# Attention steps that fill a bank of 512 score columns

## The chip, the cores and the metric

One core of a Trainium2 chip runs the whole program. The metric is device time in microseconds for one launch, the median of several executions. The engines are named as the profile names them: PE (TensorE, matrix products), PEld (its weight loads), DVE (VectorE), ACT (ScalarE), POOL (GpSimd), SP (SyncE, which issues the weight transfers).

## The reference, cut to what matters

512 tokens of width 1024 pass through two stacks of layers in float32: projections, attention, output projection, feed-forward. Four of the sublayers hold attention with heads of 64 columns, or 256 in the cross attention to a memory of 256 tokens:

```python
p = softmax(mask(q @ k.T * scale))      # per head and query: the maximum, the exponentials, their sum
o = (p * gate) @ v                      # gate: a factor per query in the first layer, else 1
```

All but the cross attention are causal: a tile `t` of 128 queries (t = 0 to 3) sees `(t + 1) * 128` keys. The first layer holds three kinds of heads: "sel" and "win" (both causal; their mixes and those of a third branch over compressed keys are added up in one bank) and "B" (a window of 128 keys, hence 128 or 256 score columns, and a sink logit that joins the sum). The second layer is causal with 16 heads, the third ("forget") causal with 8 heads and a second product that is added to the scores.

## The kernel before, in words

Each linear layer keeps 128 rows of output in a PSUM bank and adds 24 products of 128x512 for it (w_hi by x_hi, w_hi by x_lo, w_lo by x_hi, L604 to L606). Attention is a list of *steps*, made by `steps_layer0` (48 steps, called U0 here), `steps_causal` (U1 with 32 steps, UF with 16) and `steps_memory` (UX with 8, used twice). A step holds a pair of *units*, two heads with the same query tile. A unit has `nk` score columns (128 to 512), and owns one of three score banks (`S_BANKS`), one of eight buffers `pr` and a slot of `negm`, `den` and `wgt`. A *group* is all that ends up in one bank of mixes: one query tile, four pairs of heads.

The engines run the same loop, with an iteration `s` for each step and four more to drain (`TURN, LAG = 3, 4`). In iteration `s` each does the following, in this order:

- PE: scores of step s (L771), which wait until DVE has taken unit 0 of step s-1 out of its bank (`sm_done`); transposes of step s-3 (L792), which wait for POOL and for the copies of the step ahead; mixes of step s-4 (L806).
- DVE: mask and negated maximum of both units (L1721), copy of unit 0's transposes (L1731), reciprocals of the sums of step s-1 (L1735); if step s-4 ended a group, `split_mix` waits for ACT's half and writes the low part (L1701).
- ACT: exponentials of unit 0 (L1201), copy of unit 1's transposes (L1235), exponentials of unit 1; if step s-4 ended a group, `split_mix` writes the high part (L1194).
- POOL: weights the exponentials by reciprocal and gate (L566), one instruction for each unit.

`in_turns` orders the steps: wide and narrow query tiles alternate, 512 columns and then 128 (tiles 3 and 0), 384 and then 256 (tiles 2 and 1). Hooks put further work at the end of given iterations. In U0 it is the compressed branch: scores on PE (L914), mask and maximum on DVE (L1883 to L1887), exponentials on ACT (L1359), weights on DVE (L1894 to L1899), transposes on PE (L925), a copy on ACT (L1365), once for each tile, at the iterations that the `CMP_` tuples list. In UF the hooks are a conversion on ACT (L1498) and a subtraction on DVE (L2101) in iterations 4 to 7. The scores of the first two or three steps are placed into the value projection ahead (`BEGUN0`, `BEGUN`).

Of the kernel before, what the change touches and what calls it, by code (L numbers as in the profile page):

```python
# [156 lines left out]
def two_stacks(nc, x_in, mem_in, weights, small_in, tables_in, rope_in, cmpmask_in, sel_dram, out):  # L157
# [3 lines left out]
    with ctx:  # L161
# [26 lines left out]
        den = sb("den", [P, 4, 2])  # L188
        negm = sb("negm", [P, 4, 2])
        wgt = sb("wgt", [P, 4, 2])  # L190
# [159 lines left out]
        def step(group, two, opens=True, closes=True):  # L350
            return dict(group=group, two=two, opens=opens, closes=closes, begins=False, ends=False)
# [9 lines left out]
        def in_turns(couples, banks):  # L361


            steps = []
            for x, y in couples:
                assert len(x) == len(y)
                for two in zip(x, y):
                    steps += two
            for s, st in enumerate(steps):
                names = [o["group"]["name"] for o in steps]  # L370
                st["begins"] = st["group"]["name"] not in names[:s]
                st["ends"] = st["group"]["name"] not in names[s + 1:]
            free = [(0, b) for b in banks]
            n = 0
            for st in steps:
                if st["begins"]:
                    st["group"]["after"], st["group"]["bank"] = free.pop(0)
                if st["ends"]:
                    st["group"]["number"] = n
                    n += 1  # L380
                    free.append((n, st["group"]["bank"]))
            return steps
# [4 lines left out]
        def steps_layer0():  # L387
# [17 lines left out]
            def main(t):  # L405
                g = new_group(t, 0)
                return [step(g, pair(branch, t, j), branch == "sel", False)
                        for j in range(4) for branch in ("sel", "win")]

            def other(t):  # L410
                g = new_group(t, 1)
                return [step(g, pair("B", t, j)) for j in range(4)]

            return in_turns([(main(3), main(0)), (main(2), other(0) + other(1)),
                             (main(1), other(2) + other(3))], (4, 5))

        def steps_causal(q, k, v, halves, scale, banks, forget=False):
            def group(t, half):
                g = new_group(t, half)
                steps = []  # L420
                for i in range(4):
                    two, j = [], 4 * half + i
                    for b in range(2):
                        rows = slice(b * HD, (b + 1) * HD)
                        qk = [(q[rows, j, tokens(t)], k[rows, j, 0:(t + 1) * P])]
                        if forget:
# [4 lines left out]
                    steps.append(step(g, two))  # L431
                return steps

            return in_turns([(group(a, half), group(b, half))
                             for a, b in ((3, 0), (2, 1)) for half in range(halves)], banks)

        def steps_memory(banks):
            def group(t, half):
# [8 lines left out]
                return [step(new_group(t, half), two)]  # L447

            return in_turns([(group(t, 0), group(t, 1)) for t in range(TB)], banks)
# [24 lines left out]
        def ended(steps, t, half):  # L474
            return [s + 1 for s, st in enumerate(steps) if st["ends"] and st["group"]["name"] == (t, half)][0]
# [38 lines left out]
        def _(pool):  # L514
# [42 lines left out]
            def attention(steps):  # L557

                for st in steps:
                    n = pairs_seen.next() - 1  # L560
                    pool.wait_ge(wgt_ready, n + 1)
                    for a, u in enumerate(st["two"]):
                        p = pr[:, (2 * n + a) % 8, 0:u["nk"]]
                        w = wgt[:, n % 4, a:a + 1]
                        gate = ones[:, 0:1] if u["gate"] is None else u["gate"]
                        nc.gpsimd.tensor_scalar(p, p, w, gate, ALU.mult, ALU.mult).then_inc(pn_ready, 1)  # L566
# [23 lines left out]
        def _(pe):  # L590
# [170 lines left out]
            def scores(steps, s0, s):  # L761
                two = [(u, 2 * (s0 + s) + a) for a, u in enumerate(steps[s]["two"])]
                for u, n in two:
                    if n >= 3:
                        pe.wait_ge(sm_done, n - 2)

                parts = len(two[0][0]["qk"])
# [1616 lines left out]
```

## Time and profile before

| | |
|---|---|
| median of 3 runs | 2790.15 us (2788.83 to 2790.53) |
| profiled execution | 2791.02 us, its span 2789.1 us |
| PE busy in the span | 2721.9 us (98%) |
| DVE, ACT, POOL busy | 1020.7, 1099.2, 1269.6 us |
| attention phases U0, U1, UF (with their drain) | 114.2, 73.6, 41.4 us |

The span runs from the first instruction to the last; the execution's own time has 1.9 us more around it. A matmul's end is modelled in the profile and overlaps the start of the next, so a step of PE is read from the start of one kind of work to the start of the next. A float32 product of scores or mixes has two records, a transpose one.

### The profile page before, as it was taken

The page shows a single profiled execution, that of the slowest core. Times are in us where ns is not written, and L with a number is a line of the kernel's source. Part 1 is how long each engine was busy: PE and PEld are TensorE (multiplying, and loading weights), DVE is VectorE, ACT ScalarE, POOL GpSimd, SP SyncE. Part 2 cuts the span into 40 slices and gives each one's busy share as a digit, 9 for nine tenths or more (in the row PEclk, how much of TensorE's full clock was granted, in tenths as well). Part 3 has the DMA queues.
Part 4 walks back from the last instruction along what each step waited for, and adds up shares of the span by engine and source line. Part 5 has one row for each costly group of instructions (what it writes and reads, how often), then busy time and mean ns, then how long its engine had stood idle before and what let it go on. Part 6 is the DMA issues. An engine that isn't in the chain of part 4 may idle for free.

```text
span 2789.1 us, 37598 instructions
## 1 busy us (share of the span) xinstructions
PE 2721.9 (98%) x13426; PEld 2223.8 (80%) x13426; DVE 1020.7 (37%) x1931; ACT 1099.2 (39%) x1791; POOL 1269.6 (46%) x713
## 2 busy tenths in 40 slices
PE   8999999999999999999999999999999999999997
PEld 6856888888867888888868888888887788888886
DVE  5565322214544322105544335222037652422202
ACT  7565323224564333223254334323237443433321
POOL 3544444444444444444544634444444463454442
PEclk9999999999999999999999999999999999999999
DMA  4300222233211222332312412232322341132231
GB/s 165 127 2 32 90 103 92 98 106 102 98 39 50 98 98 91 105 106 76 109 42 102 146 43 83 91 104 95 108 75 99 105 153 46 62 112 98 91 109 63
DMA packets 69222, 252.08 MB, mean 90 GB/s; under 512 B 7680, under 2 KB 7936, under 8 KB 68864
## 3 DMA queue, kind: packets, MB, share of 16 engines
q1 hardware_dynamic: 68112, 247.43, 25.9%
q10 hardware_dynamic: 1008, 3.28, 0.4%
q8 instruction: 65, 1.06, 0.2%
q14 instruction: 37, 0.30, 0.0%
HBM read 248.58 MB, written 2.10 MB: 90 GB/s over the span
## 4 chain that ended last, share of the span: by engine, by line
PE 89%; DVE 6%; ACT 3%; issue 1%; DMA 0%; POOL 0%; DVEq 0%; SPq 0%; POOLq 0%; ACTq 0%
PE ps L604 25%; PE ps L605 25%; PE ps L606 25%; PE ps L771 3%; PE ps L806 3%; PE ps L792 2%; PE ps L713 1%; PE ps L715 1%; PE ps L714 1%; DVE ps L1973 1%; DVE x L1977 1%; DVE xl L1629 1%; DVE pr L1721 1%; PE ps L1013 1%; PE ps L1014 1%
## 5 line engine op out<-in xcount | busy, mean ns | idle before, releaser
L519 POOL TENSOR_TENSOR w_lo<-w_raw,w_hi 128x1024 fp32r<-128x1024 f32 x460 | 1106.7, 2410 | 1305.6 <-ACT w_hi L1133 1297.9
L604 PE MATMUL ps<-xh,w_hi 128*128 128x512 f32 x2260 | 886.7, 392 | 14.2 <-POOL w_lo L519 7.5
L605 PE MATMUL ps<-xl,w_hi 128*128 128x512 f32 x2260 | 881.6, 390 | 0.0
L606 PE MATMUL ps<-xh,w_lo 128*128 128x512 f32 x2260 | 881.3, 390 | 0.0
L1133 ACT ACTIVATE w_hi<-w_raw 128x1024 fp32r<-128x1024 f32 x462 | 485.3, 1055 | 534.3 <-PE ps L606 473.8
L604 PEld LDWEIGHTS ps<-xh,w_hi 128*128 128x128 f32 x2260 | 425.5, 188 | 110.2 <-issue 14.7
L606 PEld LDWEIGHTS ps<-xh,w_lo 128*128 128x128 f32 x2260 | 425.5, 188 | 88.7
L605 PEld LDWEIGHTS ps<-xl,w_hi 128*128 128x128 f32 x2260 | 425.6, 188 | 88.4 <-issue 1.0
L604 PE MATMUL ps<-hh,w_hi 128*128 128x512 f32 x704 | 273.9, 389 | 0.0
L606 PE MATMUL ps<-hh,w_lo 128*128 128x512 f32 x704 | 273.9, 389 | 0.0
L605 PE MATMUL ps<-hl,w_hi 128*128 128x512 f32 x704 | 273.9, 389 | 0.0
L1267 ACT ACTIVATE tmpa<-tmpa 128x512 f32<-128x512 f32 x88 | 55.6, 632 | 427.3 <-DVE tmpa L1671 427.2
L1671 DVE TENSOR_TENSOR tmpa<-ps,rstd 128x512 f32<-128x512 f32 x88 | 60.8, 690 | 385.6 <-PE ps L606 385.6
L1201 ACT ACTIVATE pr<-pr,negm 128x512 f32<-128x512 f32 (+2 forms) x224 | 120.1, 536 | 101.7 <-DVE negm L1721 101.6
L606 PEld LDWEIGHTS ps<-hh,w_lo 128*128 128x128 f32 x704 | 132.2, 188 | 27.6
L604 PEld LDWEIGHTS ps<-hh,w_hi 128*128 128x128 f32 x704 | 132.2, 188 | 27.6
L605 PEld LDWEIGHTS ps<-hl,w_hi 128*128 128x128 f32 x704 | 132.2, 188 | 27.0
L566 POOL TENSOR_SCALAR pr<-pr,wgt,ones 128x256 f32<-128x256 f32 (+3 forms) x160 | 91.3, 581 | 118.7 <-DVE wgt L1735 118.7
L1721 DVE CUSTOM_DVE_ANT_0 pr<-ps,tab 128x512 f32<-128x512 f32 (+2 forms) x192 | 85.7, 477 | 113.0 <-PE ps L771 111.7
L1671 DVE TENSOR_TENSOR tmpb<-ps,rstd 128x512 f32<-128x512 f32 x96 | 66.3, 691 | 154.5 <-PE ps L606 154.4
L1781 DVE TENSOR_TENSOR x<-ps,x 128x512 f32<-128x512 f32 x32 | 22.1, 691 | 273.0 <-PE ps L606 273.0
L1760 DVE TENSOR_TENSOR hl<-tmpb,hh 128x512 f32 (+1 forms) x88 | 63.8, 725 | 80.7 <-ACT hh L1271 80.7
(299 smaller groups left out, 2998.9 us busy)
## 6 DMA issues: line engine op xcount, KB each, us to landing
w_raw<-weights_in SPq DMA_DIRECT2D x462, 512.0 KB, 3.2
x<-x_in SPq DMA_DIRECT2D x4, 512.0 KB, 7.3
mem<-mem_in ACTq DMA_DIRECT2D x2, 1024.0 KB, 4.8
x_out<-x SPq DMA_DIRECT2D x4, 512.0 KB, 2.6
rope<-rope_in SPq DMA_DIRECT2D x1, 512.0 KB, 10.1
tab<-tables_in ACTq DMA_DIRECT2D x2, 256.0 KB, 2.7
tab<-tables_in SPq DMA_DIRECT2D x1, 384.0 KB, 10.6
small<-small_in ACTq DMA_DIRECT2D x1, 326.5 KB, 4.7
```

What stands on the lines that cost most here:

```text
L519: nc.gpsimd.tensor_tensor(w_lo[:, slot], w_raw[:, slot], w_hi.bitcast(f32)[:, slot], ALU.subtract).then_inc(lo_ready, 1)
L566: nc.gpsimd.tensor_scalar(p, p, w, gate, ALU.mult, ALU.mult).then_inc(pn_ready, 1)
L604: nc.tensor.matmul(dst, w_hi[:, slot, w], hi, start=first, stop=False)
L605: nc.tensor.matmul(dst, w_hi[:, slot, w], lo, start=False, stop=False)
L606: return nc.tensor.matmul(dst, w_lo[:, slot, w], hi, start=False, stop=last)
L771: last = nc.tensor.matmul(ps[:, S_BANKS[n % 3], 0:u["nk"]], q, k, start=c == 0, stop=c == parts - 1)
L806: last = nc.tensor.matmul(ps[rows, g["bank"], tokens(column)], values[kb], pt[:, (n + a) % 4, tokens(kb)], start=st["opens"] and kb == 0, ...
L1133: A(w_hi[:, s], w_raw[:, s], ACT.Copy).then_inc(hi_ready, 1)
L1201: A(p, p, ACT.Exp, scale=-1.0, bias=negm[:, slot, a:a + 1], accum_out=den[:, slot, a:a + 1]).then_inc(p_ready, 1)
L1671: return V.tensor_tensor(dst, bank[0:rows, 0:n], r[0:rows, 0:n], ALU.mult)
L1721: V.tensor_tensor_reduce(out=pr[:, n % 8, 0:nk], in0=ps[:, S_BANKS[n % 3], 0:nk], in1=u["mask"], scale=-u["scale"], scalar=start, op0=ALU.add,
L1760: V.tensor_tensor(at(hl), tmpb[:, j % 2], at(fp(hh)), ALU.subtract).then_inc(hl_ready, 1)
```

## The change

A step may now hold several *segments*, each a pair of units as before, laid side by side in the banks, as long as together they have at most 512 columns. Each segment keeps its own maximum, sum, reciprocal and bank of mixes, so the score products, mask-and-maximum instructions, exponentials, POOL's weightings and mixes are as many as before and as wide. The transposes of a step, the copies of them (now 512 wide for two segments), the reciprocals and the signals between engines come once for each step. `steps_causal` makes steps of tile 3 alone (512), of tiles 2 and 0 (384 + 128), and of two pairs of tile 1 (256 + 256). `steps_layer0` does the same for "sel" and "win"; "B" units stay alone, since the sink's column follows theirs. There are 37 steps in U0, 20 in U1 and 10 in UF, 29 fewer in all; UX has the same 8.

```diff
+        def step(*segs):
+            at = 0
+            for sg in segs:
+                sg["at"] = at
+                at += sg["two"][0]["nk"]
+            return list(segs)
...
-            return in_turns([(main(3), main(0)), (main(2), other(0) + other(1)),
-                             (main(1), other(2) + other(3))], (4, 5))
+            steps = [step(sg) for sg in m3]
+            steps += [step(m2[0]), step(m2[1])] + [step(m2[i + 2], m0[i]) for i in range(6)] + [step(m0[6], m0[7])]
+            for j in range(4):
+                steps += [step(b0[j]), step(m1[2 * j], m1[2 * j + 1])]
+            for j in range(4):
+                steps += [step(b1[j]), step(b2[j])]
+            return with_banks(steps + [step(sg) for sg in b3], (4, 5))
...
-            return in_turns([(group(a, half), group(b, half))
-                             for a, b in ((3, 0), (2, 1)) for half in range(halves)], banks)
+            for half in range(halves):
+                g0, g1, g2, g3 = (group(t, half) for t in range(TB))
+                for i in range(4):
+                    steps += [step(g3[i]), step(g2[i], g0[i])]
+                steps += [step(g1[0], g1[1]), step(g1[2], g1[3])]
+            return with_banks(steps, banks)
...
-        CMP_ORDER = (3, 0, 2, 1)
-        CMP_SCORES, CMP_MASKED, CMP_EXP = (1, 3, 14, 26), (1, 3, 15, 27), (1, 4, 16, 28)
-        CMP_WEIGHTS, CMP_TURNED, CMP_COPY = (1, 4, 17, 29), (2, 5, 18, 30), (2, 6, 19, 31)
+        CMP_ORDER = (3, 2, 0, 1)
+        CMP_SCORES, CMP_MASKED, CMP_EXP = (1, 4, 8, 14), (1, 4, 9, 15), (1, 5, 10, 16)
+        CMP_WEIGHTS, CMP_TURNED, CMP_COPY = (1, 6, 11, 17), (2, 7, 12, 18), (2, 8, 13, 19)
...
+                for sg in steps[s]:
+                    parts, cols = len(sg["two"][0]["qk"]), slice(sg["at"], sg["at"] + sg["two"][0]["nk"])
+                    for c in range(parts):
+                        for a, u in enumerate(sg["two"]):
+                            q, k = u["qk"][c]
+                            last = nc.tensor.matmul(ps[:, S_BANKS[(n0 + a) % 3], cols], q, k,
+                                                    start=c == 0, stop=c == parts - 1)
+                            if sg is steps[s][-1] and c == parts - 1:
+                                last.then_inc(s_ready, 1)
...
-                            for kb in range(u["nk"] // P):
+                            for kb in range(width(steps[s - TURN]) // P):
...
+                for i, sg in enumerate(steps[s]):
+                    u = sg["two"][a]
+                    p = pr[:, n % 8, sg["at"]:sg["at"] + u["nk"] + (u["sink"] is not None)]
+                    last = A(p, p, ACT.Exp, scale=-1.0, bias=negm[:, slot, i, a:a + 1],
+                             accum_out=den[:, slot, i, a:a + 1])
+                last.then_inc(p_ready, 1)
...
-                    if s >= LAG and steps[s - LAG]["ends"]:
-                        split_mix(steps[s - LAG]["group"], hi, lo)
+                    for sg in steps[s - LAG] if s >= LAG else []:
+                        if sg["ends"]:
+                            split_mix(sg["group"], hi, lo)
```

PE's queue in U1, early in the phase, before: wide and narrow steps alternate, each with its scores (L771), transposes (L792) and mixes (L806).

```order
L771 MATMUL ps<-k_r,q_r 128x512 x2
L792 MATMUL ps<-ident,pr 128x128 x2
L806 MATMUL ps<-pt,v_t 64x128 x8
L771 MATMUL ps<-k_r,q_r 128x128 x2
L792 MATMUL ps<-ident,pr 128x128 x8
L806 MATMUL ps<-pt,v_t 64x128 x2
```

The same place in the changed kernel (the lines are L793, L814 and L829 now).

```order
L793 MATMUL ps<-k_r,q_r 128x384 x2
L793 MATMUL ps<-k_r,q_r 128x128 x2
L814 MATMUL ps<-ident,pr 128x128 x8
L793 MATMUL ps<-k_r,q_r 128x512 x2
L814 MATMUL ps<-ident,pr 128x128 x8
L829 MATMUL ps<-pt,v_t 64x128 x8
```

Every run of transposes and of mixes has now eight, where it had two or eight, and a second pair of score products stands directly behind the first.

DVE's queue in U1 where the first two groups end, before: each `mix_l` stands between the reciprocals of one iteration and the mask instructions (printed as ISA) of the next, and the two ends are an iteration apart.

```order
L1731 COPY pt<-ps 128x128
L1735 RECIPROCAL wgt<-den 128x2
L1701 TENSOR_TENSOR mix_l<-ps,mix_h 128x512
L1721 ISA pr,negm<-ps,tab 128x128
L1721 ISA negm 128x1
L1721 ISA pr,negm<-ps,tab 128x128
L1721 ISA negm 128x1
L1731 COPY pt<-ps 128x512
L1735 RECIPROCAL wgt<-den 128x2
L1701 TENSOR_TENSOR mix_l<-ps,mix_h 128x512
```

The same place in the changed kernel, from the second of the ends on; tile 3's group ended an iteration earlier.

```order
L1761 COPY pt<-ps 128x512
L1765 RECIPROCAL wgt<-den 128x2
L1728 TENSOR_TENSOR mix_l<-ps,mix_h 128x512 x2
L1751 ISA pr,negm<-ps,tab 128x512
L1751 ISA negm 128x1
L1751 ISA pr,negm<-ps,tab 128x512
L1751 ISA negm 128x1
```

The groups of tiles 2 and 0 end in the same step, so two `mix_l` stand in a row ahead of the next mask instructions.

DVE's queue at the end of U1, the drain of the last steps, before: all copies of transposes (`pt`) stand ahead of the last two `mix_l`.

```order
L1731 COPY pt<-ps 128x384
L1735 RECIPROCAL wgt<-den 128x2
L1731 COPY pt<-ps 128x256
L1735 RECIPROCAL wgt<-den 128x2
L1731 COPY pt<-ps 128x384
L1731 COPY pt<-ps 128x256
L1701 TENSOR_TENSOR mix_l<-ps,mix_h 128x512 x2
```

And in the changed kernel:

```order
L1761 COPY pt<-ps 128x512
L1765 RECIPROCAL wgt<-den 128x4
L1728 TENSOR_TENSOR mix_l<-ps,mix_h 128x512
L1761 COPY pt<-ps 128x512
L1728 TENSOR_TENSOR mix_l<-ps,mix_h 128x512 x2
L1761 COPY pt<-ps 128x512
L1728 TENSOR_TENSOR mix_l<-ps,mix_h 128x512
```

The last two copies of transposes now stand behind `mix_l` instructions, where they stood ahead of them.

## Rows read from the trace of the kernel before

**Rows 1.** The page, part 4: shares of the chain that ended last, by engine.

```profile
PE 89%; DVE 6%; ACT 3%; issue 1%; DMA 0%; POOL 0%; DVEq 0%; SPq 0%; POOLq 0%; ACTq 0%
```

**Rows 2.** Stretches U0, U1, UF: us; PE, PEld, DVE, ACT, POOL busy (count); clock; DMA.

```profile
138.30:252.50 114.20, 104.73 (x943) 68.59 (x942) 78.92 (x352) 74.76 (x251) 53.30 (x94) 1.00 0.01 5
792.60:866.20 73.60, 67.53 (x601) 43.34 (x600) 46.56 (x186) 50.26 (x158) 35.85 (x60) 1.00 0.01 2
1422.30:1463.70 41.40, 35.14 (x324) 24.16 (x324) 24.93 (x90) 25.63 (x77) 16.72 (x28) 1.00 0.03 5
```

**Rows 3.** PE's waits in U0, U1, UF: sum in us, times, longest.

```profile
PE ps L771 <- DVE negm L1721: 6.1, 7, 2.0
PE ps L925 <- DVE s_c L1899: 1.2, 1, 1.2
PE ps L792 <- DVE pt L1731: 1.0, 4, 0.3
...
PE ps L771 <- DVE negm L1721: 4.6, 6, 0.9
PE ps L792 <- ACT v_t L1220: 0.4, 1, 0.4
...
PE ps L771 <- DVE negm L1721: 5.0, 6, 1.0
```

**Rows 4.** Timeline of PE in U1, without waits: start, us, instructions.

```profile
803.11 1.13 PE L771 MATMUL ps<-k_r,q_r 64*128 64x512 f32 x4
804.17 0.44 PE L792 MATMUL ps<-ident,pr 128*128 128x128 f32 x2
804.53 1.09 PE L806 MATMUL ps<-pt,v_t 128*64 128x128 f32 x16
805.56 0.49 PE L771 MATMUL ps<-k_r,q_r 64*128 64x128 f32 x4
806.04 1.07 PE L792 MATMUL ps<-ident,pr 128*128 128x128 f32 x8
807.03 0.44 PE L806 MATMUL ps<-pt,v_t 128*64 128x128 f32 x4
807.40 1.13 PE L771 MATMUL ps<-k_r,q_r 64*128 64x512 f32 x4
...
826.59 0.92 PE L771 MATMUL ps<-k_r,q_r 64*128 64x384 f32 x4
827.44 0.44 PE L792 MATMUL ps<-ident,pr 128*128 128x128 f32 x2
```

**Rows 5.** Timeline of U1 where the first group ends: start, us, [idle <-releaser].

```profile
809.86 0.49 PE L771 MATMUL ps<-k_r,q_r 64*128 64x128 f32 x4
...
810.29 0.71 ACT L1201 ACTIVATE pr<-pr,negm 128x512 f32<-128x512 f32 x1
...
810.99 0.58 ACT L1194 ACTIVATE mix_h<-ps 128x512 fp32r<-128x512 f32 x1
...
811.33 0.44 PE L806 MATMUL ps<-pt,v_t 128*64 128x128 f32 x4
811.61 0.69 DVE L1701 TENSOR_TENSOR mix_l<-ps,mix_h 128x512 fp32r<-128x512 f32 x1 [1.35 <-ACT mix_h L1194]
812.21 0.28 DVE L1721 CUSTOM_DVE_ANT_0 pr<-ps,tab 128x128 f32<-128x128 f32 x1
...
812.65 1.13 PE L771 MATMUL ps<-k_r,q_r 64*128 64x512 f32 x4 [0.88 <-DVE negm L1721]
```

**Rows 6.** ACT's exponentials in U1 by shape: xcount | busy us, mean ns | idle.

```profile
L1201 ACT ACTIVATE pr<-pr,negm 128x384 f32<-128x384 f32 x16 | 9.7, 609 | 8.1 <-DVE negm L1721 8.1
...
L1201 ACT ACTIVATE pr<-pr,negm 128x128 f32<-128x128 f32 x13 | 5.1, 392 | 1.0 <-DVE negm L1721 1.0
```

**Rows 7.** Timeline of U0, compressed branch: DVE's weights, then PE's transposes.

```profile
149.01 0.42 DVE L1894 TENSOR_REDUCE cst<-s_c 128x8 f32<-128x256 f32 x1 [1.17 <-ACT s_c L1359]
...
150.59 0.44 PE L925 MATMUL ps<-ident,s_c 128*128 128x128 f32 x2 [1.24 <-DVE s_c L1899]
```

More of the change, by code:

```diff
@@ L359, in tokens, with with_banks @@
             return slice(t * P, (t + 1) * P)
[L361 to L372, printed above, removed]
+        def with_banks(steps, banks):
+            segs = [sg for st in steps for sg in st]
+            names = [sg["group"]["name"] for sg in segs]
             free = [(0, b) for b in banks]
             n = 0
[L375 to L379, printed above, removed]
+            for s, sg in enumerate(segs):
+                sg["begins"] = names[s] not in names[:s]
+                sg["ends"] = names[s] not in names[s + 1:]
+                if sg["begins"]:
+                    sg["group"]["after"], sg["group"]["bank"] = free.pop(0)
+                if sg["ends"]:
+                    sg["group"]["number"] = n
                     n += 1
-                    free.append((n, st["group"]["bank"]))
+                    free.append((n, sg["group"]["bank"]))
             return steps
@@ L446, in group @@
                     two.append(unit(qk, MEM, tab[:, 0:MEM], 1 / 16, places))
-                return [step(new_group(t, half), two)]
-            return in_turns([(group(t, 0), group(t, 1)) for t in range(TB)], banks)
+                return step(seg(new_group(t, half), two))
+            return with_banks([group(t, half) for t in range(TB) for half in range(2)], banks)
         U0 = steps_layer0()
@@ L474, in ended @@
         def ended(steps, t, half):
-            return [s + 1 for s, st in enumerate(steps) if st["ends"] and st["group"]["name"] == (t, half)][0]
+            return [s + 1 for s, st in enumerate(steps) for sg in st
+                    if sg["ends"] and sg["group"]["name"] == (t, half)][0]
         block = ctx.enter_context(nc.Block())
@@ L561, in attention @@
                     pool.wait_ge(wgt_ready, n + 1)
[L562 to L566, printed above, removed]
+                    for a in range(2):
+                        for i, sg in enumerate(st):
+                            u = sg["two"][a]
+                            p = pr[:, (2 * n + a) % 8, sg["at"]:sg["at"] + u["nk"]]
+                            w = wgt[:, n % 4, i, a:a + 1]
+                            gate = ones[:, 0:1] if u["gate"] is None else u["gate"]
+                            last = nc.gpsimd.tensor_scalar(p, p, w, gate, ALU.mult, ALU.mult)
+                        last.then_inc(pn_ready, 1)
             pool.wait_ge(lo_ready, FIRST_TILES)
@@ L785, in attention @@
                     if TURN <= s < len(steps) + TURN:
-                        for a, u in enumerate(steps[s - TURN]["two"]):
+                        for a in range(2):
                             n = 2 * (s0 + s - TURN) + a
@@ L815, in attention @@
                         hook()
-                mts.n += 1 + max(st["group"]["number"] for st in steps)
+                mts.n += 1 + max(sg["group"]["number"] for st in steps for sg in st)
             pe.wait_ge(pool_set, 1)
@@ L929, in cmp_transposes, with cmp_values @@
                 return run
-            def cmp_values(st):
-                g = st["group"]
+            def cmp_values(sg):
+                g = sg["group"]
                 i = CMP_ORDER.index(g["t"])
                 pe.wait_ge(cmp_copied, i + 1)
-                for a, u in enumerate(st["two"]):
+                for a, u in enumerate(sg["two"]):
                     rows, j, _ = u["places"][0]
@@ L1230, in copy_turned @@
                         n = 2 * (s0 + s - TURN) + 1
-                        nk = steps[s - TURN]["two"][1]["nk"]
+                        nk = width(steps[s - TURN])
                         act.wait_ge(pt_ready, n + 1)
```

111 lines of the change are left out of this document (56 added, 55 removed).

## The prediction

> **What bounds the kernel now.** I read the chain first: 89% of it is PE's [rows 1], so an engine that gets less to do brings nothing unless PE had waited for it. Then the three stretches in which the change acts. They last 114.2 + 73.6 + 41.4 = 229.2 us, 8% of the span [rows 2]; nothing outside them is touched. In each, DVE, ACT and POOL are busy for 40 to 69% of the time (in U1 46.6, 50.3 and 35.9 of 73.6 us), no weights stream, and the clock is at its full level of 2.4 GHz [rows 2], so neither bandwidth nor clock enters. The waits of PE say what it waits for: 6.1 + 1.2 + 1.0 us in U0, 4.6 + 0.4 in U1, 5.0 in UF, 18.3 us in 25 waits [rows 3]. Modelled ends hide a piece of each: PE's mixes of one block that start at 811.33 would have been over after 0.37 us (so long they take at 807.03), at 811.70, and the next scores start at 812.65, 0.95 us late, where the row shows 0.88 idle [rows 4, 5]. With 0.07 to 0.08 for each of 25, PE loses about 20.3 us.
>
> Where PE doesn't wait, its own sequence sets the pace. A wide and a narrow step take 803.11 to 807.40, 4.29 us, with no idle time [rows 4]. Differences of starts give the pieces: scores of 512 columns 1.06, of 384 0.85, of 128 0.48; transposes of four blocks 0.99, of one 0.36; mixes of four blocks 1.03, of one 0.37 [rows 4].
>
> **Turns.** Three further blocks of transposes cost 0.99 - 0.36 = 0.63, so 0.21 each, and 0.15 of a run is fixed; mixes likewise (0.66 for three, 0.15 fixed). These fixed parts are PE's turn from one kind of work to the next, with its waits. A merged pair of segments has one run of transposes and one of mixes instead of two: 0.30 us less for each of 29 steps that go, 8.7 us. Scores save nothing: each segment brings its own products, 0.85 + 0.48 before and after. Order doesn't alter a sum: the wider second step, whose scores now lengthen the value projection ahead, takes nothing that it didn't take elsewhere.
>
> **Waits at the end of a group.** At 809.86 the group's last mixes give way to the next scores. ACT still does the exponentials of unit 1 (810.29 to 810.99), then mix_h until about 811.57; DVE, held behind it, does mix_l from 811.61 and the next mask from 812.21; at 812.65 PE may go on: 2.79 us [rows 5]. PE had work for one step meanwhile, a narrow one of 1.84 us. The changed kernel has steps of 1.06 + 0.99 + 1.03 = 3.1 us (one segment) or 0.85 + 0.42 + 2.02 = 3.3 us (two). After a step with one segment the same chain, with a mask of 512 instead of 128 columns, is covered.
>
> Two things speak against. First, ACT is later in a step with two segments: its exponentials take 609 + 392 ns for a unit [rows 6] instead of 0.71 us for 512 columns at once [rows 5], 0.28 more, 0.56 for both units, and DVE's two masks add about 0.1. Secondly, two groups end together, which adds a mix_h (0.58, about 0.5 start to start) and a mix_l (0.60) [rows 5]. I lay the queues down from these durations. In U1 the first end (tile 3, behind one segment) is covered but leaves DVE and ACT 0.6 us late. In the next iteration, counted from PE's first scores: mask of unit 0 out at 2.9 instead of 2.3, its exponentials to 4.0, copy to 4.5, exponentials of unit 1 to 5.5, two mix_h to 6.6, the second mix_l to 7.4, the next mask (512) to 8.1. PE wanted that after its own 3.3 and 3.1 us, at 6.4: about 1.8 us with the signals. Tile 1's end, behind two segments, by the same count: 0.55. In the drain the copy of the last transposes stands behind two mix_l; these end 2.05 us after the mixes, the copy at 2.7, and PE has 2.0 us of work: 0.7. The second half's ends all fall into the drain. U1 then waits 3.1 us where it waited 4.6 + 0.4 (v_t, covered now by 1.33 us of scores instead of 0.48) and small ones.
>
> In UF all ends fall into the drain (0.7). There the hooks of iterations 4 to 7 act like an end of a group: DVE waits for ACT behind its exponentials. The first is covered, the other three cost 1.1, 0.7 and 1.4, since each starts late from the one ahead: 3.9 us in all against 5.0 plus small ones.
>
> U0, in order: 0.6 at the start as now; 1.0 in iteration 8, where PE's compressed scores need the copy pc_t, which the tuples put into the same iteration behind ACT's exponentials (mask out at 0.85 + 0.22 + 0.55, exponentials 0.6, copy 0.5, exponentials 0.6, copy 0.4: 3.8 to 3.9, against 2.9 of PE's work); 1.8 in iteration 12, where PE's turned weights need DVE's chain of 1.6 us (149.01 to 150.59 [rows 7]) that stands behind tile 3's mix_l; 1.85 after tile 0's end, since a step of 128 columns follows; 0.85 after tile 1's; 1.15 and 1.0 in the drain. The wait of 1.2 us for s_c [rows 3, 7] is gone, with two iterations more in between. Sum 8.2.
>
> After: 8.2 + 3.1 + 3.9 = 15.2. Before: 20.3, and 1.2 for a handful of waits of 0.3 and less: 21.5. Gain 6.3 us. This is the soft term. Below, I bound it by no gain (every end waits as now), above by all 21.5.
>
> **Others.** POOL keeps its instructions, 35.9 us of them [rows 2] in some 66 us of U1, so it has room. A step's weightings are now done for both segments before one signal; the transposes they feed are three steps later, some 9 us after the scores, and mask, exponentials, reciprocal and weighting take about 7.5. DVE and ACT lose 29 copies and 29 reciprocals each or between them, which nothing waits for. The masks of a second segment write other columns of the same bank, the same instructions as now.
>
> The Trainium skill, "Trainium Kernel Development and Optimization", Best Practices, says that tiling speeds up compute but not the evacuation of PSUM; here that would mean that merging cannot help an attention that DVE and ACT pace. By that rule the sum would be near zero; the trace doesn't bear it out, as both are idle for about a third of each stretch [rows 2]. What it would take is rival (d).
>
> **Sum.** 8.7 + 6.3 = 15.0 us. The profiled execution took 2791.0 us (span 2789.1 and 1.9 around it), 0.9 above the median of 2790.15. The forecast is 2790.15 - 15.0 = 2775.1, rounded to 2775.
>
> **Rivals.**
> (a) Only the turns are saved: the longer chain of ACT and DVE eats what the wider steps cover. For it: two ends in one step, three hooks in a row in UF. Against: the narrow steps behind each end are gone in U1. Then 2790.2 - 8.7, with waits up to 2 us either way: 2779.5 to 2783.5. 20%.
> (b) Nearly all waits go: the queues recover faster than I laid down, two thirds of 21.5 us or more. 2790.2 - 8.7 - 14 or more: 2767.5 and below, to 2760. 12%.
> (c) The turns aren't saved: PE's fixed 0.15 is a matter of something else than of the run, and stays. Against it: runs of one and of four blocks in the same stretch give it for transposes and mixes alike [rows 4]. Only the waits then: 2790.2 - 6.3 = 2784, and no change if the waits stay too. 5%, of which 3% within 0.2%. The TensorE page of the Trainium skill (TensorE: Matmul & The Clock Gate, Back-to-back issue gap) gives one spacing for a stream of loads and products by their width, with no price for a turn; by that rule the first term would be nothing.
> (d) Slower: ACT becomes the pace. One iteration with two segments costs it 2 x (0.61 + 0.39) for the exponentials [rows 6] and a copy of about 0.6, 2.6 us against PE's 3.3. It decides once ACT needs over 3.3 + 0.3, the saved turn, which would take half a microsecond more for each extra exponential than its row has; at 4.1 us the 29 steps with two segments lose 0.8 each, 23 us, and the turns give 8.7 back: 2804. 4%.
> My own forecast, waits between 9 and 19 us: 2769 to 2779. 59%.
>
> **Numbers.** Below 2766 lies about half of (b), above 2783 lie (d), (c) and the edge of (a), in all some 17%: the range is 2766 to 2783; the forecast's own is 2769 to 2779. A measurement of this kernel tells about 0.2% (5.6 us) from no change. Faster by more: 0.93; within: 0.04; slower: 0.03.
>
> **What would show it.** In the trace after: PE's starts in a step of 384 + 128 columns 0.85 + 0.45, 0.99, 1.03, and U1's 20 steps 3.6 us shorter in PE's own work; PE's waits for negm at two places in U1 (about 1.8 and 0.5), three in UF, a wait for pc_t in U0's iteration 8 and for s_c in iteration 12; a wait for the copy pt in each drain. The stretches U0, U1, UF about 109.5, 66.5 and 37 us (now 114.2, 73.6, 41.4). Wrong would be: transposes waiting for POOL in every iteration, exponentials back to back on ACT (then d), or waits for negm in each of the ends (then a).

## The result and the profile after

| | before | after |
|---|---|---|
| time, median (lowest to highest) | 2789.8 us (2788.8 to 2790.5) | 2824.6 us (2821.4 to 2827.0) |
| profiled execution, span | 2789.1 us | 2821.8 us |
| PE busy | 2721.9 us | 2763.1 us |

The changed kernel is slower: 1.0123 times the time of before, with an interval of 1.0110 to 1.0136. The forecast was 2775 us, the range ended at 2783.

I look first where the change acts. The three attention phases from their first scores to their last mixes, in the windows view of the kernel before (us; busy time and count of PE, PEld, DVE, ACT, POOL; granted clock; DMA):

```profile
124.50:250.88 126.38, 117.43 (x1031) 80.80 (x1029) 85.17 (x377) 78.31 (x261) 59.12 (x98) 1.00 0.03 10
773.08:864.72 91.64, 85.99 (x682) 56.92 (x681) 48.61 (x198) 59.01 (x175) 45.42 (x67) 1.00 0.07 24
1402.30:1462.00 59.70, 53.96 (x410) 38.12 (x409) 26.92 (x102) 33.88 (x94) 26.27 (x35) 1.00 0.10 35
```

And of the changed kernel:

```profile
123.03:245.19 122.16, 113.34 (x1031) 83.28 (x1029) 82.04 (x356) 77.29 (x250) 59.93 (x98) 0.99 0.03 10
780.38:863.34 82.96, 79.97 (x682) 58.41 (x681) 46.20 (x175) 57.57 (x163) 45.21 (x67) 1.00 0.08 26
1413.46:1468.47 55.01, 51.09 (x410) 38.63 (x409) 25.97 (x91) 32.97 (x88) 27.08 (x35) 1.00 0.11 38
```

They are 4.2 + 8.7 + 4.7 = 17.6 us shorter, a little more than the 15.0 of the forecast. So the loss, 32.7 us of span, lies elsewhere, and it must be about 50 us. Between the phases the same instructions run: U1 begins 7.3 us later although U0 ended 5.7 us earlier. The costliest groups on the page of the changed kernel (busy us, mean ns of one, idle) show where:

```profile
L626 PE MATMUL ps<-xh,w_hi 128*128 128x512 f32 x2260 | 899.4, 398 | 12.6 <-POOL w_lo L538 7.3
L628 PE MATMUL ps<-xh,w_lo 128*128 128x512 f32 x2260 | 898.5, 398 | 0.0
L627 PE MATMUL ps<-xl,w_hi 128*128 128x512 f32 x2260 | 883.6, 391 | 0.0
...
L626 PE MATMUL ps<-hh,w_hi 128*128 128x512 f32 x704 | 279.1, 397 | 0.0
```

On the page of before the same lines read:

```profile
L604 PE MATMUL ps<-xh,w_hi 128*128 128x512 f32 x2260 | 886.7, 392 | 14.2 <-POOL w_lo L519 7.5
L606 PE MATMUL ps<-xh,w_lo 128*128 128x512 f32 x2260 | 881.3, 390 | 0.0
...
L604 PE MATMUL ps<-hh,w_hi 128*128 128x512 f32 x704 | 273.9, 389 | 0.0
```

These are the dense linear products, whose code the change doesn't touch. Their count is the same and their idle time is no longer than before; each simply takes longer. Since matmuls overlap, I measure the distance from one product's start to the next. PE's timeline of the changed kernel in a dense stretch (start, us):

```profile
999.86 0.40 PE L626 MATMUL ps<-xh,w_hi 128*128 128x512 f32 x1
1000.09 0.39 PE L627 MATMUL ps<-xl,w_hi 128*128 128x512 f32 x1
1000.32 0.40 PE L628 MATMUL ps<-xh,w_lo 128*128 128x512 f32 x1
...
1001.95 0.39 PE L626 MATMUL ps<-xh,w_hi 128*128 128x512 f32 x1
```

Nine products in 2.09 us are 232 ns each. Over the whole trace the medians behind the three kinds of product (xh with w_hi, xl with w_hi, xh with w_lo) are 234, 230 and 235 ns, where before had 227, 227 and 226. Summed over every pair of neighbouring dense products the distances grow from 2383.8 to 2436.2 us: 52.4 us. 52.4 - 17.6 - 1.5 (the first scores start 1.5 us earlier) = 33.3, against 32.7 in the spans. The account closes to 0.6 us.

The granted clock over the span is 0.993 and 0.994, the mean DMA rate 90 and 89 GB/s: neither accounts for 50 us. What does differ for these products is where their operands lie. The diff makes den, negm and wgt 32 bytes longer each, and all buffers allocated behind them (xh, y_dn, hh, hl, mix_h, pr, pt and the rest, but not x, w_raw, w_hi, w_lo and xl) move up by 96 bytes per partition. In the program built from before, xh lies at 121984 and w_hi at 49280, a distance of 142 x 512; in the changed one it is 96 more.

### The profile page after: what moved, and what is told of

The parts are those of the page before. It is cut to its first block, busy times and chain, and to the rows that moved or that the text cites. A ratio compares the mean times of both kernels' runs of the same rounds, so it can differ in the third digit from the quotient of the medians.

```text
span 2821.8 us, 37279 instructions
## 1 busy us (share of the span) xinstructions
PE 2763.1 (98%) x13426; PEld 2226.9 (79%) x13426; DVE 1008.7 (36%) x1873; ACT 1093.8 (39%) x1762; POOL 1272.0 (45%) x713
## 3 DMA queue, kind: packets, MB, share of 16 engines
q8 instruction: 65, 1.06, 0.2%
## 4 chain that ended last, share of the span: by engine, by line
PE 90%; DVE 5%; ACT 3%; issue 1%; DMA 0%; POOL 0%; DVEq 0%; SPq 0%; POOLq 0%; ACTq 0%
PE ps L626 26%; PE ps L628 26%; PE ps L627 25%; PE ps L793 3%; PE ps L829 2%; PE ps L814 2%; PE ps L735 1%; PE ps L736 1%; PE ps L737 1%; PE ps L1037 1%; PE ps L1038 1%; PE ps L1036 1%; ACT pr L1226 1%; DVE pr L1751 0%; DVE ps L2004 0%
## 5 line engine op out<-in xcount | busy, mean ns | idle before, releaser
L626 PE MATMUL ps<-xh,w_hi 128*128 128x512 f32 x2260 | 899.4, 398 | 12.6 <-POOL w_lo L538 7.3
L628 PE MATMUL ps<-xh,w_lo 128*128 128x512 f32 x2260 | 898.5, 398 | 0.0
L1226 ACT ACTIVATE pr<-pr,negm 128x384 f32<-128x384 f32 (+5 forms) x224 | 119.5, 535 | 89.7 <-DVE negm L1751 89.7
L1751 DVE CUSTOM_DVE_ANT_0 pr<-ps,tab 128x384 f32<-128x384 f32 (+3 forms) x192 | 83.4, 476 | 106.2 <-PE ps L793 105.5
```

The source lines that it names most:

```text
L626: nc.tensor.matmul(dst, w_hi[:, slot, w], hi, start=first, stop=False)
L628: return nc.tensor.matmul(dst, w_lo[:, slot, w], hi, start=False, stop=last)
L1226: last = A(p, p, ACT.Exp, scale=-1.0, bias=negm[:, slot, i, a:a + 1], accum_out=den[:, slot, i, a:a + 1])
L1751: last = V.tensor_tensor_reduce(out=pr[:, n % 8, cols], in0=ps[:, S_BANKS[n % 3], cols], in1=u["mask"], scale=-u["scale"], scalar=start, o ...
```

## The experiments

Theory A: the places of the buffers slow the dense products. Rivals: B, the changed program's instructions are fetched otherwise; C, the shorter attention shifts the weight stream against the products. All experiments but the last two are about this. A *grain* is the number of bytes of which a shift must be a multiple to cost nothing. The distances behind each product are collected in one table below.

### e1 to e4: shifts of 128, 96, 64 and 32 bytes

e1 is the changed kernel, e2 to e4 the kernel before, each with one unused tile. For e2:

```
         stat = sb("stat", [P, 3, TB])
+        pad = sb("pad", [P, 24])
```

e1 has `[P, 8]`, e3 `[P, 16]`, e4 `[P, 4]`. In the built programs every buffer starts at a multiple of 32 bytes, so e4's tile of 16 bytes moves xh and all behind it by 32 (xh lies at 122016): e4 tests a shift of 32 bytes, and no run tests one of 16.

> The changed kernel with one unused tile of 32 bytes per partition allocated behind stat, so that every buffer behind it (xh, hh, hl, pr, mix_h and the rest) stands 128 bytes, not 96, beyond its place in the kernel before; no instruction is added. Theory A (the 32-byte shift of these buffers against multiples of 64 slows the dense products: 227 ns from one product's start to the next became 231 to 237): the products return to 226 to 227 ns, the roughly 50 us they lost come back, and the time is about 2772 to 2776 us, near the 2775 of the prediction. Theory B (the changed program's instructions stand elsewhere and are fetched otherwise) and theory C (the shorter attention shifts the weight stream against the products): nothing of that is touched, the time stays at 2821 to 2827 us and the spacing at 231 to 237 ns.

> The kernel before with one unused tile of 96 bytes per partition behind stat, which puts xh and all buffers behind it at the places they have in the changed kernel; no instruction differs. Theory A: the products slow to 231 to 237 ns apart and the time rises by what the changed kernel lost outside attention, 34.8 + 18 = about 50 us: 2835 to 2845 us. Theories B and C: 2789 to 2791 us, no change.

> The kernel before with an unused tile of 64 bytes behind stat: the buffers behind it move, but each keeps its place against multiples of 64. Theory A with a grain of 64 bytes: no change, 2790 us, products 227 ns apart. Theory A with a grain of 128 bytes: slower, by up to 50 us. Theories B and C: 2790 us.

> The kernel before with an unused tile of 16 bytes behind stat. Theory A with a grain of 32 or 64 bytes: slower, by about as much as with 96 bytes (2835 to 2845 us). If only a grain of 16 bytes or less counts: 2790 us. Theories B and C: 2790 us.

Measured: e1 2801.5 us (1.0046 of before, 1.0031 to 1.0060), e2 2845.2 (1.0207, 1.0190 to 1.0224), e3 2848.8 (1.0216, 1.0196 to 1.0237), e4 2836.8 (1.0173, 1.0153 to 1.0194). An unused tile of 96 bytes makes the kernel before over 50 us slower, without any other instruction: B and C are out as the main cause. The page of e2 has the product lines of the changed kernel, to the nanosecond:

```profile
L605 PE MATMUL ps<-xh,w_hi 128*128 128x512 f32 x2260 | 899.0, 398 | 12.2 <-POOL w_lo L520 6.4
L607 PE MATMUL ps<-xh,w_lo 128*128 128x512 f32 x2260 | 898.5, 398 | 0.0
L606 PE MATMUL ps<-xl,w_hi 128*128 128x512 f32 x2260 | 883.7, 391 | 0.0
```

But my theory of multiples of 64 is wrong. A shift by 64 costs as much as one by 96, and the changed kernel at 128 regains less than half (23 us). A grain of 32, 64 or 128 bytes is out with e4, e3 and e1; it is coarser. (The forecast for e4 took its shift for one of 16 bytes.)

### e5: the changed kernel with every other buffer in its old place

```
-        den = sb("den", [P, 4, 2, 2])
+        den_gap = sb("den_gap", [P, 4, 2])
...
+        den = place("den", [P, 4, 2, 2], 88.25)
```

The same for negm and wgt (88.5 and 88.75).

> The changed kernel with den, negm and wgt moved to free memory behind all other buffers, and gaps of their old size left in their old places, so that every other buffer stands exactly where it stands in the kernel before. Same instructions as the changed kernel. Theory A2 (the places of the product operands against each other or against some coarser grain set the spacing of the dense products, and not whether they are multiples of 64 bytes): the spacing is 226 to 227 ns again and the time is the span of before, 2789.1, less the 17.7 us that the three attention stretches gained, so 2771 to 2774 us. Rival B (the changed program's code slows the products): spacing 231 to 237 ns and 2822 us, or with a part of both something between, above 2780.

Measured: 2770.1 us, 0.9933 of before (0.9920 to 0.9947). The instructions of the changed kernel in the old places gain 20.6 us. The products are as before:

```profile
L630 PE MATMUL ps<-xh,w_hi 128*128 128x512 f32 x2260 | 885.1, 392 | 14.1 <-POOL w_lo L542 7.9
L632 PE MATMUL ps<-xh,w_lo 128*128 128x512 f32 x2260 | 880.4, 390 | 0.0
...
L630 PE MATMUL ps<-hh,w_hi 128*128 128x512 f32 x704 | 273.9, 389 | 0.0
```

and its timeline has six products in 1.36 us, 227 ns each:

```profile
1000.10 0.39 PE L630 MATMUL ps<-xh,w_hi 128*128 128x512 f32 x1
...
1001.46 0.39 PE L630 MATMUL ps<-xh,w_hi 128*128 128x512 f32 x1
```

Rival B gets nothing: summed, the distances between dense products are 2379.7 us, where before had 2383.8. Of the 20.6 us the three phases account for 15.9 in the profiled executions; most of the rest (4.9 us) lies ahead of the first scores, a stretch that took 119.6 us here and 124.5 in before, but 120.0 in e10, which has the instructions of before.

### e6 to e8: one region alone, all together, 512 bytes

In the kernel before: e6 has 96 unused bytes behind y_dn (only hh, hl, mix_h, pr and their region move), e7 64 bytes ahead of x (all buffers move), e8 512 bytes behind stat.

```
         y_dn = sb("y_dn", [P, KT, T])
+        pad = sb("pad", [P, 24])
```

> The kernel before with 96 unused bytes between y_dn and the region of hh: xh keeps its place, hh, hl, mix_h, pr and everything in that region move by 96 bytes. Theory A2, with the effect tied to the operand that moved: the xh and xl products stay at 226 to 227 ns (their sum 1544 us), the hh, hl, mix and y products go to 231 to 237 ns, which costs 6 us a group of hh and hl times three less some, about 14 us, and 2 to 3 us for mix and y: 2804 to 2808 us. If instead any move of any buffer unsettles all products: 2835 us or more.

> The kernel before with 64 unused bytes ahead of x: all buffers move by 64 bytes together, so their distances from each other stay. With 64 bytes behind stat alone the time had been 2848.8 us. If the distance between the moving operand and the weights (or the two read streams against each other) counts: 2790 us, 227 ns. If the place itself against a fixed grain of the memory counts: slower, up to 2849 us.

> The kernel before with 512 unused bytes behind stat. With a grain of 512 bytes or a divisor of it that is at least 256: 2790 us. With a coarser grain, or none (the spacing follows the whole place): slower, between 2800 and 2850 us.

Measured: e6 2806.4 us (1.0059, 1.0040 to 1.0077), e7 2790.6 (1.0000, 0.9990 to 1.0010), e8 2789.6 (0.9997, 0.9987 to 1.0007). On e6's page the x products keep their time and those of hh don't:

```profile
L605 PE MATMUL ps<-xh,w_hi 128*128 128x512 f32 x2260 | 885.2, 392 | 14.3 <-POOL w_lo L520 7.8
...
L607 PE MATMUL ps<-hh,w_lo 128*128 128x512 f32 x704 | 280.9, 399 | 0.0
L606 PE MATMUL ps<-hl,w_hi 128*128 128x512 f32 x704 | 277.4, 394 | 0.0
```

So the effect stays with the products whose operand moved. Moving everything by 64 costs nothing where moving a part by 64 costs some 60 us: for this shift it is the distance between buffers that counts, not the place itself.

### e9, e10, e13, e15: which distances, and the grain

In the kernel before: e9 has 96 bytes between w_hi and w_lo, e13 96 bytes between w_raw and w_hi, e15 96 bytes ahead of w_lo and 160 behind it, e10 256 bytes behind stat. e15:

```
+        pad = sb("pad", [P, 24])
         w_lo = sb("w_lo", [P, RING, CW], f32r)
+        pad2 = sb("pad2", [P, 40])
```

> The kernel before with 96 unused bytes between w_hi and w_lo: w_lo, xl, xh, hh, hl and all the rest move together, so they keep their distances (multiples of 512 bytes) to w_lo and lose them to w_hi. Theory D (a product is slowed where the weights loaded for the next product stand off a multiple of 512 from the moving operand that streams meanwhile): the spacing behind the xh product with w_hi is slow (231 to 237 ns: the next load is from w_hi), behind the xl product 227 (the next load is from w_lo), behind the xh product with w_lo slow. Rival E (a product's own weights and moving operand count): slow behind both products with w_hi, 227 behind the one with w_lo. Either way two of three products are slowed: 2820 to 2840 us. If neither distance counts: 2790 us.

> The kernel before with 256 unused bytes behind stat; 512 had left the time as it was and 128 had left 28 us of loss in the changed kernel. A grain of 256 bytes: 2790 us, products 227 ns apart. A grain of 512 bytes: slower, between 2800 and 2850 us.

> The kernel before with 96 unused bytes between w_raw and w_hi: w_hi, w_lo, xl, xh, hh, hl and all the rest move together; x and w_raw stay. If only the distances among what TensorE reads count: 2788 to 2792 us, products 227 ns apart. If the distance from w_raw to w_hi and w_lo counts (ScalarE and GpSimd read one and write the other all the time): slower, up to 2845 us.

> The kernel before with 96 unused bytes ahead of w_lo and 160 behind it: only w_lo stands off, everything behind it has moved by 256. Theory D (the weights loaded for the next product against the operand that streams meanwhile): slow only behind the xl product with w_hi, 8 us of loss or less for xl and hl together with 2964 products of 3 to 7 ns: 9 to 20 us, 2800 to 2810 us. Rival E (a product's own weights): slow only behind the xh product with w_lo, the same 9 to 20 us. Rival F (any operand off its place slows all three, since each product's start depends on the one ahead): all spacings above 229 ns, 2815 to 2845 us.

Measured: e9 2831.5 us (1.0153, 1.0134 to 1.0171), e10 2790.7 (1.0007, 0.9996 to 1.0017), e13 2790.8 (1.0002, 0.9992 to 1.0012), e15 2839.7 (1.0179, 1.0159 to 1.0200). Median distance in ns from the start of one product to the start of the next, behind each kind, computed from all of them in each trace:

| kernel | moved against w_hi | xh·w_hi | xl·w_hi | xh·w_lo | hh·w_hi | hl·w_hi | hh·w_lo |
|---|---|---|---|---|---|---|---|
| before | nothing | 227 | 227 | 226 | 227 | 226 | 227 |
| after | xh, hh, hl: 96 | 234 | 230 | 235 | 233 | 237 | 231 |
| e2 | the same | 235 | 230 | 235 | 233 | 237 | 231 |
| e1 | the same, 128 | 232 | 226 | 228 | 232 | 232 | 232 |
| e3 | the same, 64 | 233 | 232 | 231 | 233 | 234 | 233 |
| e4 | the same, 32 | 235 | 232 | 232 | 233 | 234 | 234 |
| e6 | hh, hl: 96 | 227 | 226 | 227 | 231 | 231 | 238 |
| e5, e7, e13 | nothing | 227 | 226-227 | 227 | 226-227 | 226-227 | 227 |
| e8, e10 | xh, hh, hl: 512; 256 | 227 | 226-227 | 227 | 226-227 | 227 | 227 |
| e9 | all others: 96 | 232 | 231 | 231 | 232 | 231 | 231 |
| e15 | w_lo: 96; xl, xh, hh, hl: 256 | 233 | 232 | 233 | 233 | 232 | 232 |

The products run 227 ns apart whenever all that PE reads (w_hi, w_lo, xl, xh, hh, hl) lies multiples of 256 bytes apart (differences of 0, 256 and 512 to the distances of before were tried), and some or all kinds of them slower in every case in which one of these buffers doesn't. e13 says that x and w_raw, which only the converting engines read, don't count, and again that a common shift, of 96 bytes here, is free. Theories D (the load of the next weights) and E (a product's own weights) both expected one slow kind in e15; all six are slow, even the product of xh with w_hi, whose own weights and those loaded for the next product both lie right, and the loss is 51 us, where both had expected 9 to 20. That is what F expected: the whole train of products is slow. Its reason, that each product starts from where the one ahead had left off, is not shown. Nor is the train slow evenly: in e1 the xl products keep 226. On e15's page:

```profile
L606 PE MATMUL ps<-xh,w_hi 128*128 128x512 f32 x2260 | 900.7, 399 | 12.7 <-POOL w_lo L521 7.3
L608 PE MATMUL ps<-xh,w_lo 128*128 128x512 f32 x2260 | 893.0, 395 | 0.0
L607 PE MATMUL ps<-xl,w_hi 128*128 128x512 f32 x2260 | 891.0, 394 | 0.0
```

Which product of three is slow isn't fixed by its kind either. With hh and hl off by 96 bytes, one of the three takes 237 or 238 ns and the others 230 to 232: in the changed kernel it is hl·w_hi in the first two down projections and hh·w_hi in the last two (the medians 233 and 237 of the table mix the two), in e6 hh·w_lo in all. The three together take 700 ns in both, against 680 before. So an offset sets the time of a round of three, and the table's columns shouldn't be read as prices of single kinds; e15 refutes D and E by the size of the loss, not by the columns alone.

The inside of it stays open. The distances behind the products of xh with w_lo have a median of 235 ns in every tenth of the changed kernel, while other engines come and go. That speaks for something between PE's own streams (moving operand and weights) rather than for a collision with ScalarE, GpSimd or DMA, but no run shows it by itself.

### e14: the changed kernel with one line of repair

160 unused bytes behind stat, so that the shift is 256 and not 96.

```
         stat = sb("stat", [P, 3, TB])
+        pad = sb("pad", [P, 40])
```

> The changed kernel with 160 unused bytes behind stat, so that all buffers behind it stand 256 bytes beyond their places of before, where 96 is what the change alone moves them by. With a grain of 256 bytes: products 227 ns apart and 2769 to 2774 us, as with every buffer in its old place. If the changed kernel needs the old places themselves: 2780 us or more.

Measured: 2772.7 us, 0.9937 of before (0.9921 to 0.9954), products 227 ns apart. This is the change as it should be shipped; from 2824.6 us the unused tile brings 52.

### e12: the segments of U1 and UF as steps of their own

On the base of e5:

```
-                    steps += [step(g3[i]), step(g2[i], g0[i])]
-                steps += [step(g1[0], g1[1]), step(g1[2], g1[3])]
+                    steps += [step(g3[i]), step(g2[i]), step(g0[i])]
+                steps += [step(g1[i]) for i in range(4)]
```

> The changed kernel with every buffer in its place of before, but with the segments of U1 and UF as steps of their own in the same order (18 steps more: 12 in U1, 6 in UF); U0 stays merged. Theory as in the prediction (0.15 us of a run of transposes and 0.15 of a run of mixes are fixed, scores save nothing): PE's own time rises by 18 x 0.30 = 5.4 us, waits by up to 2.5: 2775 to 2778 us. What the traces of both kernels point to instead (the turn from scores to transposes costs about 0.3 as well, 0.52 for a step in all): PE's own time rises by 6.3 us in U1 and 3.1 in UF, the whole is 2779 to 2783 us.

Measured: 2791.9 us (1.0009 of before, 1.0000 to 1.0019), 21.8 over e5; both forecasts were too low. Its windows of U1 and UF, first scores to last mixes:

```profile
771.07:865.59 94.52, 88.94 (x682) 58.56 (x681) 48.78 (x199) 59.05 (x175) 45.31 (x67) 0.96 0.07 24
1402.86:1465.30 62.44, 56.74 (x410) 40.11 (x409) 27.31 (x103) 33.84 (x94) 26.31 (x35) 0.95 0.10 34
```

against e5's:

```profile
765.64:848.48 82.84, 79.85 (x682) 58.41 (x681) 46.20 (x175) 57.57 (x163) 45.21 (x67) 1.00 0.08 27
1385.71:1440.63 54.92, 51.02 (x410) 38.67 (x409) 25.99 (x91) 32.97 (x88) 27.06 (x35) 1.00 0.10 38
```

11.7 and 7.5 us longer. PE's listed waits take 5.2 + 5.4 us, where e5 has 2.8 + 3.9. The granted clock is the third part: e12's trace has it at half, 1.2 instead of 2.4 GHz, for 2 x 3.4 us in U1 and for 6.8 us in UF, which cost about half of that, 3.4 each; e5's has it at full there. What remains is 11.7 - 2.4 - 3.4 = 5.9 for 12 steps and 7.5 - 1.5 - 3.4 = 2.6 for 6: 0.47 us a step. That supports the measured price of a turn below, and not the 0.30 of the prediction. The clock had been in neither forecast. Since the order of the groups also differs from before, the comparison is with e5 alone. The two windows hold 19.2 us of the difference; the profiled executions also differ by 4.8 us ahead of the first scores, where the programs don't.

### e11: hooks of the compressed branch one iteration later

On the base of e5:

```
-        CMP_SCORES, CMP_MASKED, CMP_EXP = (1, 4, 8, 14), (1, 4, 9, 15), (1, 5, 10, 16)
-        CMP_WEIGHTS, CMP_TURNED, CMP_COPY = (1, 6, 11, 17), (2, 7, 12, 18), (2, 8, 13, 19)
+        CMP_SCORES, CMP_MASKED, CMP_EXP = (1, 4, 9, 15), (1, 4, 10, 16), (1, 5, 11, 17)
+        CMP_WEIGHTS, CMP_TURNED, CMP_COPY = (1, 6, 12, 18), (2, 7, 13, 19), (2, 8, 14, 20)
```

> The changed kernel with every buffer in its place of before, as in the run that took 2770 us, and the third and fourth set of compressed-branch hooks one iteration later (scores, mask, exponentials, weights, turn and copy in 9 to 14 and 15 to 20, where they stood in 8 to 13 and 14 to 19). Theory: PE's wait of 0.9 us for pc_t goes (scores and copy no longer share iteration 8), the wait of 1.4 + 0.3 us for s_c goes (the weights no longer stand behind mix_l of tile 3), and with them the fall of the granted clock to 0.5 for 3.4 us behind the second, 1.7 us: U0 takes 119.5 to 121 us from its first scores to its last mixes (now 124.0; 122.1 in the run without the clock's fall in the drain), the whole 2765 to 2768 us. Rival: the waits only move, since DVE and ACT are late all the same: some 2770 us.

Measured: 2770.7 us (0.9936, 0.9923 to 0.9950), not to be told from e5. In the trace U0 did shrink as expected, to 120.4 us, and the clock holds:

```profile
123.85:244.25 120.40, 111.97 (x1031) 82.17 (x1029) 82.98 (x356) 76.93 (x250) 59.47 (x98) 1.00 0.03 10
```

PE's waits there:

```profile
PE ps L797 <- DVE negm L1755: 5.1, 6, 1.5
PE ps L818 <- DVE pt L1765: 3.0, 4, 1.6
```

The waits for pc_t and s_c are gone, but a wait of 1.5 us for negm stands at the end of tile 3's group in their place: DVE is as late as ever behind mix_l. The sum of these waits fell only from 9.0 (e5) to 8.1 us. So the rival was half right: the waits moved. This U0 is 1.8 us shorter than the changed kernel's and 3.6 shorter than e5's. Nearly all of that is the clock, which stood at half for 3.4 us in the one and for 2 x 3.4 us in the other (1.7 and 3.4 us lost), and that the moved hooks are what kept it up isn't shown (below, e14 keeps it without them). For the whole these differences are too small, because executions differ by more than that before the first scores even start (at 119.6 us in e5's trace, at 123.9 in this one). Whether the whole gains by it is unclear.

## Why the prediction was wrong

**The step that failed** is the sentence "nothing outside them is touched". The larger den, negm and wgt moved every buffer behind them by 96 bytes against the weights; the dense products went from 227 to 230 to 237 ns apart and lost 52.4 us (e2 shows the loss without the change, e5 the change without the loss). No rival had it. Nothing in the trace of before would have given the price, but the order of allocation was in the diff, and PE's 98% busy time should have made me ask what could touch the products.

**Stretches.** With the product loss taken out, the forecast of 2775 stands against 2770.1 (e5) and 2772.7 (e14), the gain of 15.0 us against 20.6 and 16.3. The stretches of [rows 2], shifted to the changed kernel's own phases, were forecast at 109.5, 66.5 and 37 us:

```profile
136.83:246.81 109.98, 100.81 (x947) 71.89 (x946) 75.37 (x330) 72.15 (x239) 53.41 (x94) 0.98 0.01 5
799.90:864.82 64.92, 61.56 (x601) 44.90 (x600) 42.64 (x158) 47.71 (x143) 35.83 (x61) 1.00 0.02 7
1433.46:1470.17 36.71, 32.43 (x322) 24.85 (x321) 22.41 (x74) 23.76 (x68) 17.58 (x29) 1.00 0.03 8
```

**Turns: right in kind, too small.** "Scores save nothing" was wrong. PE's timeline of the changed kernel in U1, without waits, against [rows 4]:

```profile
824.94 1.14 PE L793 MATMUL ps<-k_r,q_r 64*128 64x384 f32 x8
826.01 1.09 PE L814 MATMUL ps<-ident,pr 128*128 128x128 f32 x8
827.03 1.09 PE L829 MATMUL ps<-pt,v_t 128*64 128x128 f32 x16
828.06 1.13 PE L793 MATMUL ps<-k_r,q_r 64*128 64x512 f32 x4
```

Transposes and mixes take 1.02 and 1.03, as forecast. But the scores of 384 + 128 columns take 1.07 from start to start, where I had put 0.85 + 0.45 = 1.30 (the prediction uses 0.48, 0.42 and 0.45 for the second part in three places; its row gives 0.48). The price of 0.48 for 128 columns in [rows 4] already held a turn of about 0.23 (1.30 - 1.07) to the transposes, just as the others do; I had separated it for two of the three kinds only, because the rows offered two widths with the same number of blocks and I read the scores' 1.06, 0.85 and 0.48 as prices of width. That makes 0.30 + 0.23 = 0.53 us a step. From the phases: U1's 8.7 us less some 2.5 of waits leave 6.2 for 12 steps, UF's 4.7 less 1.7 leave 3.0 for 6, 0.51 us a step. The term was about 29 x 0.53 = 15.4 us, not 8.7; for U0's 11 steps the price is carried over.

**Waits: right in place, gain too large.** The changed kernel's waits in U0, U1 and UF:

```profile
PE ps L793 <- DVE negm L1751: 3.4, 4, 1.5
PE ps L814 <- DVE pt L1761: 2.9, 3, 1.6
PE ps L948 <- DVE s_c L1930: 1.4, 1, 1.4
PE ps L937 <- ACT pc_t L1392: 0.9, 1, 0.9
...
PE ps L793 <- DVE negm L1751: 1.8, 2, 1.6
PE ps L814 <- DVE pt L1761: 0.5, 2, 0.3
PE ps L829 <- DVE pt L1761: 0.5, 1, 0.5
...
PE ps L793 <- DVE negm L1751: 3.1, 3, 1.1
PE ps L829 <- DVE pt L1761: 0.5, 1, 0.5
PE ps L814 <- DVE pt L1761: 0.3, 1, 0.3
```

One by one: 0.89 for pc_t (forecast 1.0), 1.36 + 0.34 for s_c (1.8), 1.47 and 1.04 behind the ends of tiles 0 and 1 (1.85 and 0.85), 1.56 + 0.92 in the drain (1.15 + 1.0); in U1 1.62 behind the double end (1.8) and 0.16 (0.55), in UF 1.01, 0.94, 1.11 (1.1, 0.7, 1.4). The list of queues laid down by hand held nearly everywhere. The rows sum to 15.3 us and, with the 0.07 hidden behind each of 19, to some 16.6. The gain against 21.5 is 4.9, not 6.3.

**The clock: a term that was missing.** The wait for s_c did more than last 1.4 us. The windows around it in the changed kernel (PE's busy time first, the clock before the last two):

```profile
174.00:176.00 2.00, 0.64 (x8) 0.22 (x4) 1.86 (x9) 0.00 (x0) 0.00 (x0) 1.00 0.00 0
176.00:177.90 1.90, 1.54 (x12) 1.15 (x12) 1.75 (x11) 1.62 (x6) 0.31 (x1) 0.99 0.00 0
177.90:181.30 3.40, 3.40 (x25) 2.74 (x25) 1.90 (x10) 3.40 (x14) 3.25 (x7) 0.51 0.00 0
```

PE stood still for 1.36 and 0.34 us within 3 us, and then worked for 3.4 us at 1.2 GHz: eight transposes take 1.62 from start to start instead of 1.02, twelve mixes likewise longer. That costs 1.7 us of U0 and is why U0 gained only 4.2: 11 x 0.53 = 5.8 of turns, waits about even, less 1.7.

The pause alone doesn't bring the fall, though. e14 runs the same instructions and has the same waits of 1.36 and 0.34 us at this place, and its clock stays at full behind them, with 38 records of PE in 3.4 us instead of 25:

```profile
173.60:175.60 2.00, 0.64 (x8) 0.25 (x4) 1.86 (x9) 0.00 (x0) 0.00 (x0) 1.00 0.00 0
177.60:181.00 3.40, 3.40 (x38) 2.68 (x36) 2.35 (x13) 3.40 (x14) 3.25 (x7) 1.00 0.00 0
```

In the same way the drain's waits of 1.56 and 0.92 us left the clock at full in the changed kernel and were met by 3.4 us at half in e5 and e14, and the kernel before has a wait of 1.96 us in U0 at full clock. e11 has 1.00 throughout, but so has e14 at that place. In the traces of the changed kernel, e1, e5 and e14 one or two such falls lie in the attention phases, in eight of the eleven traces of the kernel before and its padded forms none. What decides between them no run shows; the term belongs into a forecast as a range, from nothing to some 4 us.

15.4 + 4.9 - 1.7 = 18.6, against 17.6 measured in the phases. The forecast of 15.0 for them came out close by luck: one term was too small, another too large, and a third missing.

**The rivals.** (a), (b), (c) and (d) are all about the attention. (c) is refuted by e12: the turns are real. (d) didn't come: ACT is busy for 57.6 of 83.0 us in U1. The forecast ended on the wrong side by a mechanism that stood in none of them.

## What to carry to other kernels

When a change resizes any buffer, compare the addresses of all buffers before and after and keep the distances between everything that PE reads, here up to multiples of 256 bytes; 160 unused bytes were worth 52 us of 2825, more than twice what the change itself brings (16 to 21). Where two kernels differ in time outside the edited part, compare the start-to-start distances of identical instructions, and test the placement by adding an unused tile to the kernel before. And price a turn between kinds of work on PE for every kind in the cycle: merging two steps into one saved 0.53 us, 0.23 of it at the scores, where I had looked for nothing.

## What the runs showed of the hardware that was not expected

- Dense fp32r products of 128x128 weights and 512 columns start every 227 ns when w_hi, w_lo and the moving operands lie multiples of 256 bytes apart per partition, and every 226 to 238 ns when they don't (32, 64, 96 and 128 bytes tried; three products together 687 to 700 ns instead of 680). A common shift of all buffers by 64 bytes (e7), or of all that PE reads for them by 96 (e13), changes nothing.
- One operand off its place slows the products that don't read it, too, if they stand in the same train (e15), while products of another stretch keep their 227 ns (e6).
- Short pauses of PE, 1.4 + 0.3 us within 3 us, were followed by 3.4 us at 1.2 GHz in one execution, 1.7 us lost besides the pause itself, and by none in another with the same instructions and pauses (e14). In e12 the clock's mean was 0.96 over U1 and 0.95 over UF, and such falls cost some 7 of the 19 us by which it is longer there.
